# Cached attention, recurrent branch and the split of the mixed activations, moved into the 72 attention slots

## The reference, cut to what matters

```
fox:  p = softmax(q k^T / 8 + f_q - f_k)              out = p v
sb :  w = exp(log_sigmoid(z) + sum of log_sigmoid(-z) over the later keys)   out = w v
lru:  xc = conv4(xr);  r, i = sigmoid(xc W_r + b_r), sigmoid(xc W_i + b_i)
      a = exp(8 r log_sigmoid(lam));  h = a h + sqrt(1 - a^2) i xc;  y = h gelu(xg)
mix = concat(fox, sb, lru) @ w_out;   layer norm;   ConvFFN;   layer norm
```

## Time and profile before

| | us |
|---|---|
| median of 3 runs | 1707.6 (1703.89 to 3819.81) |
| the profiled execution | 1707.65, its span 1706.0 |
| mean granted clock of PE | 0.951 |
| PE busy | 1549.5 (91%) |
| DVE busy | 845.8 (50%) |
| ACT busy | 370.8 (22%) |
| POOL busy | 248.2 (15%) |

### The profile page before, as it was taken

One profiled execution on the slowest core, in us unless ns is written; L12 is line 12 of the kernel. 1 busy time (PEld: TensorE's weight loads), 2 busy tenths in 40 slices (PEclk: granted clock), 3 DMA queues, 4 the chain that ended last, 5 costly groups with the idle time before them and its releaser, 6 DMA issues.

```text
span 1706.0 us, 26008 instructions
## 1 busy us (share of the span) xinstructions
PE 1549.5 (91%) x9907; PEld 1367.7 (80%) x9907; DVE 845.8 (50%) x1187; ACT 370.8 (22%) x597; POOL 248.2 (15%) x166
## 2 busy tenths in 40 slices
PE   5898999998999974999977999999999999999894
PEld 3767777776778762339976999999999999999894
DVE  3314556685555448163363444444444445544556
ACT  2212233333554431121332211001100010000011
POOL 0001443443222221330121000000000000000004
PEclk9899998988999986999997999999999999999997
DMA  9664554453010004874110110121111211121112
GB/s 347 205 216 103 148 150 129 137 158 106 26 51 25 1 1 138 263 222 125 38 52 23 49 46 29 49 61 49 34 38 56 58 37 31 56 62 37 46 56 87
DMA packets 175860, 151.24 MB, mean 89 GB/s; under 512 B 19051, under 2 KB 156983, under 8 KB 175778
## 3 DMA queue, kind: packets, MB, share of 16 engines
q1 hardware_dynamic: 143434, 123.35, 23.7%
q10 hardware_dynamic: 28256, 14.26, 3.0%
q0 software_dynamic: 4096, 12.59, 2.4%
HBM read 139.37 MB, written 10.91 MB: 88 GB/s over the span
## 4 chain that ended last, share of the span: by engine, by line
PE 64%; issue 15%; DVE 7%; SPq 4%; POOL 3%; ACT 3%; DMA 2%; POOLq 1%; ACTq 0%; DVEq 0%
PE ps L1879 41%; PE ps L1887 8%; PE ps L1660 6%; PE ps L1737 2%; PE ps L1755 2%; PE ps L1712 2%; POOL k_page L714 2%; SPq L599 2%; PE ps L1839 2%; SPq L603 1%; SPq L601 1%; DVE scores L816 1%; DMA k_page<-in_cache_fox_k 1%; DVE ln_st L1104 1%; DVE pr L890 1%
## 5 line engine op out<-in xcount | busy, mean ns | idle before, releaser
L1879 PE MATMUL ps<-acts_hi,w_hi 128*128 128x344 f32 x1056 | 225.0, 322 | 3.0 <-DVE acts_lo L1179 3.0
L1879 PE MATMUL ps<-acts_lo,w_hi 128*128 128x344 f32 x1056 | 224.9, 321 | 0.0
L1879 PE MATMUL ps<-acts_hi,w_lo 128*128 128x344 f32 x1056 | 223.6, 320 | 0.0
L1660 PE MATMUL ps<-acts_hi,w_hi 128*128 128x344 f32 (+1 forms) x552 | 189.7, 344 | 9.1 <-issue 3.2
L1660 PE MATMUL ps<-acts_lo,w_hi 128*128 128x344 f32 (+1 forms) x552 | 182.8, 331 | 0.0
L1660 PE MATMUL ps<-acts_hi,w_lo 128*128 128x344 f32 (+1 forms) x552 | 182.4, 331 | 0.0
L1879 PEld LDWEIGHTS ps<-acts_hi,w_hi 128*128 128x128 f32 x1056 | 178.4, 189 | 3.1 <-issue 3.1
L1879 PEld LDWEIGHTS ps<-acts_lo,w_hi 128*128 128x128 f32 x1056 | 179.5, 190 | 0.0
L1879 PEld LDWEIGHTS ps<-acts_hi,w_lo 128*128 128x128 f32 x1056 | 176.7, 189 | 0.0
L1061 DVE CAST w_hi<-w_raw 128x1024 fp32r<-128x1024 f32 x72 | 49.7, 691 | 255.3 <-PE ps L1879 249.6
L714 POOL TENSOR_TENSOR k_page<-k_page,q_row 128x1536 f32<-128x1536 f32 x32 | 112.9, 3529 | 146.5 <-DMA k_page<-in_cache_fox_k 81.9
(11 more groups left out here) (310 smaller groups left out, 2543.0 us busy)
## 6 DMA issues: line engine op xcount, KB each, us to landing
w_raw<-in_w_up SPq DMA_DIRECT2D x44, 512.0 KB, 3.8
w_ada<-in_w_ada SPq DMA_DIRECT2D x10, 2048.0 KB, 8.0
k_page<-in_cache_fox_k SPq DMA_DIRECT2D x64, 192.0 KB, 2.4
k_page<-in_cache_sb_k SPq DMA_DIRECT2D x64, 192.0 KB, 2.5
v_page<-in_cache_sb_v POOLq DMA_DIRECT2D x64, 192.0 KB, 3.7
v_page<-in_cache_fox_v SPq DMA_DIRECT2D x64, 192.0 KB, 3.7
w_raw<-in_w_in ACTq DMA_DIRECT2D x15, 512.0 KB, 5.2
w_raw<-in_w_down SPq DMA_DIRECT2D x16, 384.0 KB, 3.2
```

The costliest lines, as they stand in the source:

```text
L1660: last = nc.tensor.matmul(bank[0:cols, 0:CH], w[:, n % 2, k, 0:cols], a[:, k, c * CH:(c + 1) * CH], start=k == 0 and w is w_hi and a is ac ...
L1879: last = nc.tensor.matmul(proj_ps[half][:, c, 0:CH], w[:, half, k], a[:, k, c * CH:(c + 1) * CH], start=k == 0 and w is w_hi and a is hi, ...
```

## The change

- `q_row` has one buffer. The query row of request r waits for both products of request r-1 (`s_km` at 2r+4 where it was 2r+2).
- The sb reductions stand in slots 18 to 29, four in three slots, where they were one to a slot in 18 to 33.
- The softmaxes of the cached scores are made on 128 rows (keys) by small PE jobs and DVE and ACT steps in slots 17 to 24 (fox) and 30 to 33 (sb).
- The cached values are 16 PE jobs `v0` to `v15`, one at the end of each slot 33 to 48. A job has 8 matmuls whose weights are 6 columns wide, on four column groups of 32. SP loads the 8 pages of a job into `k_page`; the loads of job n wait until job n-1 is done.
- The input tiles of the recurrent branch come in another order, and the last 18 dense thirds stand in slots 49 to 66, one in each. The recurrent branch runs in slots 52 to 72.
- The high parts of the mixed tiles are written by ACT as it empties the values; the low parts are taken by DVE, sent to memory (`mix_scr`) and, when the last dense third is done, loaded with the high parts into `acts_hi` and `acts_lo` by SP.
- All small jobs and dense thirds share `ps_dense` and one count (`JOB`): each waits until the one ahead of it has been emptied.
- The masks are added by one matmul for each head in place of two.

```diff
-        for r in range(2 * NB):
-            RED_AT.setdefault(max(first_sb, 2 * NB) + r, []).append(2 * NB + r)
+        SB_K = 18
+            RED_AT.setdefault(SB_K + 3 * r // 4, []).append(2 * NB + r)
+        SB_Z = SB_K + 12
+        V_AT = SB_Z + 3
+        NVU = 2 * 2 * NPG // 2
+        G0, G1 = LATE + 5, LATE + 14
+        for n in range(NVU):
+            AFTER[V_AT + n] = "v%d" % n
...
+        LATE = 4 * UP + 1
+        X1_AT = LATE + 12
+        for k, g in enumerate([*range(LATE, LATE + 12), *range(X1_AT, X1_AT + 6)]):
+            SLOT_DENSE[g] = [at + k]
...
+            def k_pages(b, kind):
                 r = NB * kind + b
-                sp.wait_ge(s_km, 2 * r + 2)
+                sp.wait_ge(s_km, 2 * r + 4)
                 row = sq_scr[ds(b, 1), kind * W:kind * W + W].to_broadcast([P, W])
-                sp.dma_start(q_row[:, j], row).then_inc(s_ql[j], 16)
+                sp.dma_start(q_row[:], row).then_inc(s_ql, 16)
                 for half in range(2):
-                    sp.wait_ge(s_kfree, 2 * r + half + 1)
+                    sp.wait_ge(s_kf[half], r + 1)
...
+            def v_pages(n):
+                kind, bg, pp = n // 8, n // 4 % 2, n % 4
+                for half in range(2):
+                    if n:
+                        sp.wait_ge(s_pm, JOB["v%d" % (n - 1)] + 1)
+                    else:
+                        sp.wait_ge(s_kf[half], 2 * NB + 1)
+                    for x in range(4):
+                        page = page_of(4 * bg + x, 2 * pp + half)
+                        sp.dma_start(k_page[:, half, x, 0:W], vpools[kind][ds(page, 1)]...).then_inc(s_kl[half], 16)
...
+            def values_products(n):
+                for half in range(2):
+                    pe.wait_ge(s_kl[half], 64 * (2 * NB + 4 * grp + pp + 1))
+                    for x in range(4):
+                        last = nc.tensor.matmul(ps_dense[32 * x:32 * x + H, 0:cols], p_all[:, 2 * pp + half, 4 * bg + x],
+                                                k_page[:, half, x, 0:cols], start=half == 0, stop=half == 1 and not own)
...
+            def aux(name):
+                pe.wait_ge(s_pe, JOB[name])
...
+                    if g == at + 4:
+                        dve.wait_ge(r_s, 2 * t + 4)
+                        rstep(V.tensor_scalar(r, r, -1.0, 1.0, ALU.mult, ALU.add))
+                        rstep(V.reciprocal(r, r))
+                        rstep(V.tensor_tensor(x, x, r, ALU.mult))
...
+            def mix_low(n):
+                dve.wait_ge(v_h, n + 1)
+                V.tensor_tensor(mix_lo[:], ps_val, qT[:, t, half], ALU.subtract).then_inc(v_e, 1)
...
+            sp.wait_ge(s_pm, DENSE_END)
+            for t in range(NP2):
+                sp.wait_ge(s_ms, 16 * min(2 * t + 2, 2 * NP2 - 1))
+                sp.dma_start(acts_hi[:, t, 0:n].bitcast(F32), qT[:, t, 0:n]).then_inc(s_mx, 16)
+                sp.dma_start(acts_lo[:, t, 0:n].bitcast(F32), mix_scr[t, :, 0:n]).then_inc(s_mx, 16)
```

More of the change, by code:

```diff
@@ L398, in hybrid_step @@
         at = PRE
-        for ph in range(NP2):
+        for ph in range(4):
             m = NCH * PHASES[ph + 1]
@@ L906, in _ @@
+            dve.sem_inc(g_ws, 2)
+            for g in range(NU + LAG):
+                decode_step(g)
+                if g in LO_AT:
+                    mix_low(LO_AT[g])
                 if 1 <= g <= HALF_U and ends(g - 1):
@@ new lines, in after_values, with decode_step @@
+            def after_values(g):
+                name = AFTER.get(g)
+                if name in ROWS:
+                    rows_out(name)
+                elif name == "lru":
+                    lru_out()
+                elif name and name[0] in "ri":
+                    gate(name)
+            def decode_step(g):
+                if g == 22:
+                    act.wait_ge(s_pe, JOB["level"] + 1)
+                    A.activation(z_fox, z_fox, ACT.Exp).then_inc(d_a, 1)
+                    A.activation(d_small[:, 2:3], d_small[:, 1:2], ACT.Exp, bias=d_small[:, 0:1]).then_inc(d_a, 1)
+                if g == SB_Z:
+                    act.wait_ge(d_d, DV["clip"])
+                    A.activation(sp_flat, sp_flat, ACT.Exp).then_inc(d_a, 1)
+                    act.wait_ge(d_a, 3)
+                    A.activation(sp_flat, sp_flat, ACT.Ln, bias=1.0).then_inc(d_a, 1)
+                if g == SB_Z + 3:
+                    act.wait_ge(s_pe, JOB["tail"] + 1)
+                    A.activation(z_sb, z_sb, ACT.Exp).then_inc(d_a, 1)
@@ L1719, in scores_of @@
                     at = qb % 4 * P
-                    for e in range(2):
-                        for hd in range(2):
-                            r = slice(HD * hd, HD * hd + HD)
-                            last = nc.tensor.matmul(bank[:, hd, at:at + P], sel2[r, e], mk[r, 0 if fox else 1, e], start=False, stop=e == 1)
+                    for hd in range(2):
+                        last = nc.tensor.matmul(bank[:, hd, at:at + P], ident_r[:], mk[:, 0 if fox else 1], start=False, stop=True)
                 last.then_inc(f_s, 1)
@@ L1757, in values @@
                 last.then_inc(v_m, 1)
+            def values_products(n):
+                grp, pp = n // 4, n % 4
+                kind, bg = grp // 2, grp % 2
+                cols = W + 1 - kind
+                p_all = scores[:, kind]
+                if n in (0, 8):
+                    pe.wait_ge(d_a, 2 if n == 0 else 5)
+                own = kind == 0 and pp == 3
+                for half in range(2):
+                    pe.wait_ge(s_kl[half], 64 * (2 * NB + 4 * grp + pp + 1))
+                    for x in range(4):
+                        last = nc.tensor.matmul(ps_dense[32 * x:32 * x + H, 0:cols], p_all[:, 2 * pp + half, 4 * bg + x], k_page[:, half, x, 0:cols],
+                                                start=half == 0, stop=half == 1 and not own)
+                if own:
+                    for x in range(4):
+                        b = 4 * bg + x
+                        last = nc.tensor.matmul(ps_dense[32 * x:32 * x + H, 0:cols], d_self[:, b * H:b * H + H], smp_rows[0:NB, 0:cols],
+                                                start=False, stop=True)
+                return last
```

836 lines of the change are left out of this document (449 added, 387 removed).

## The result

The changed kernel takes **1790.3 us** (median of 4, 1787.1 to 1791.8) against 1705.8 (median of 4) in the runs beside it: ratio 1.0497, 95% interval 1.0478 to 1.0515. One of those four runs took 3819.8 us; the other three lie between 1703.9 and 1707.6. It is slower by 84.6 us; the forecast was 1772, with slower as the likeliest side. The profiled execution of the changed kernel has a span of 1790.0 us and a mean granted clock of 0.915 (before 1706.0 and 0.951), so its own ledger adds up to +84.0.

The account below looks back on a forecast made before the run. The prediction took the cached keys' loop of loads, at SP's rate, to pace slots 0 to 15, with PE alone busy after the slots. Terms -133 + 74 + 98 + 24 + 1 = +64 on 1707.65 us gave 1772 us, range 1680 to 1806.

Parts of the forecast that it names:

- Removed block: After the slots: of 135.5 us between last values and output projection, 2.6 us stay, mixed tiles' loads hidden; net -133 us.
- Fox keys: Slots 0 to 15: one query row puts landing and product between requests, 21.8 us each; +38 us.
- Stick-breaking keys: Now slots 18 to 29: requests take 15.7 us each; cumulative loss +74 us at slot 34, stage itself +36 us.
- the ring: Cached keys' loop of SP's issues, landing, POOL's product and DVE's reduction; said to pace slots 0 to 15 already.
- Value jobs: Slots 33 to 48: issues, landing and second-half matmuls follow one another, 12.0 us a period; +98 us.
- PE has room there: Slots 0 to 48: more time at the lower clock expected, but a 7 us slot at half rate stays under 12.
- slower still: Rival, value jobs: matmuls on the four column groups do not overlap, 28 us more, 1800 us; chance 0.13.
- Transfer-bound: Rival, value and sb pages: SP's issues do not count, eight pages take 4.5 us, not 8.2; 1687 us; chance 0.12.
- Hidden pages: Rival, key and value loads: they overlap with the slots, so PE sets every slot; 1629 us; chance 0.13.
- Slots 49 to 66: Four more dense thirds (15.8 us), the gates (7.4) and sample rows (0.7) add time; +24 us.
- Last slots: Slots 67 to 71: DVE sets the end; its idle time swallows 11.4 of 12.2 us added, reciprocal at 2.3; +1 us.
- After the block: From output projection to the kernel's end: no change, 0 us.

## Why the forecast was right on the side and 18 us low

*Removed block: right.* 1.9 us stay, 2.6 were put; the loads of the mixed tiles were hidden.

*Fox keys: right, somewhat dear.* 21.0 us a request against 21.8; slot 16 opens at 316.4 where I had put 323 or after; +32.4 against +38. Taking away the single row gives back all of it. The steps that the change adds under this ring cost nothing, as put: with two rows slots 0 to 15 take 120.8 us, 122.2 before.

*Stick-breaking keys: right in size.* 16.1 us a request against 15.7, slot 34 at 474.9 against 479. But I gave it all to the ring. With two rows only 12.5 of its 37 us come back, so about two thirds of the stage's loss have another cause than the single row: 9.3 us of more work on PE, and waits that this study did not part further. That the sum came out near is partly luck.

*Value jobs: the failed term.* The mechanism stood (issue, landing, matmuls, one after another), and its size was off: 13.2 us a job in place of 12.0, which is 18 of the 19 us of the stage's error. The means of the fifteen jobs, term by term, from SP's and PE's timelines:

| term of a period | put | measured |
|---|---|---|
| job's end to the first issue | 0.8 | 0.8 |
| first to last of eight issues | 8.18, less 0.2 for written-out code | 7.9 |
| last issue to PE's use of the page | 2.5 | 2.9 |
| the second half's four matmuls | 0.72 | 1.34 |
| the sample's own matmuls, two jobs only | 0 | 0.1 |

The matmuls are half of the 1.2 us. They take 0.83 at 2.4 GHz and 1.47 at 1.2, and twelve of the fifteen second halves ran at the lower level, after PE had stood 2.5 to 5.4 us for the pages; the other three stood 1.2 to 3.0 us. In the stage without loads the clock is 0.92 in place of 0.77. I had seen the clock and costed it at nothing in the sum: "PE has room there" holds for the slot's other work, but these matmuls stand on the path. (The rival "slower still" names half rate, and gives it no price of its own.) Another third is the landing: twelve jobs took 2.5 to 2.8 us, three 3.5 to 4.8, and why these three were slow no run parts.

*Transfer-bound: wrong here.* The rival took the issues as free. Two queues bring 33 us, so they are not; but the landing of a page rises from 2.5 to between 3.4 and 3.8 when two queues issue at once, so there is something in it.

*Hidden pages: half an answer.* Its 1629 took 1.5 us for a job and nothing for DVE. The stage without loads is 127 us, not 82 + 24 = 106: 5 more is work of PE beside the jobs, and 16 is idle time that came up behind the loads, in which the waits for DVE's adds are nearly all that PE stands (19.5 of 21.0 us). That wait was not in the forecast.

*Slots 49 to 66: right.* +26.5 against +24, PE the bound at a clock of 0.99.

*Last slots: too cheap.* +8.9 in place of +1. The reciprocal took 6.60 us where my bounds were 0.8 and 2.3, 4.3 us over the value taken. By the Trainium skill (VectorE: DVE Perf Modes, First, the fixed hardware budget) the reciprocal repeats its divide step 8 times, from which my estimate was 8.6 us. The measured 6.60 is nearer to that than to the 2.3 that I took, but 2 us less; eight times the one-operand pass of the earlier trace rows, 0.82, would have been 6.5. The other half: I let DVE's idle time before its products, 11.4 us, swallow the added passes. It swallowed a part only, since the idle time stands before the scan in the order of work and the recurrence stands ahead of it; PE's turn, ACT's emptying and the next scores follow one by one, at a clock of 0.62 (0.86 in these slots before).

*After the block: -4.6 us that I had at 0.* No run was made on it, and it stays open. In all other versions this part took 929 to 932 us, also in the kernel before with one query row (931.7), which has the kernel before's code there; so at least 2 of the 4.6 us need no change in the code.

The errors: value jobs +18.9, last slots +7.9, slots 49 to 66 and the block +1.9, slot 0 +0.5, keys -4.6, after the block -4.6: the 20 us between +64 and +84. The total is nearer than its terms, since 29 us put too low and 9 put too high stand against each other.

## What to carry to other kernels

Before work is moved under slots that have "room", write down the loop that its loads make (who releases the buffer, how long the issues take one after another, the landing, the work that releases again) and compare its period with the slot; with space for one job that period is the slot. A second buffer for something as small as a query row can be worth more (49 us here) than the space it gives. And cost the short work that stands at the end of each wait at the lower clock: here it ran so in twelve of fifteen jobs.

## What the runs showed that I had not expected

- An fp32 reciprocal of 128x1032 on DVE took 6.60 us, 6.4 ns an element of the row; other one-operand passes over that length took 0.68 to 0.81 in the same kernel, two-operand passes 1.23.
- One or four matmuls of 128x6 against 385 columns on their own column groups cost the stage the same: 127.2 and 127.4 us.
- Issuing pages from a second queue raised the time from issue to landing from 2.5 us to 3.4 and 3.6 on SP's queue and 3.7 and 3.8 on POOL's (sb and fox pages); a POOL issue mostly occupied it for 0.54 to 0.58 us, one every 1.15 us with the page number's read.
